# Last attention of a two-block kernel: who merges the dilated groups' weights, and when queries are squared

## The reference

```python
DILATED_GROUPS = ((128, 1), (512, 4), (2048, 16))   # window, dilation
q = rms_norm(h, norm_g) @ w_in                       # 4 heads x 3 groups of 128
q = apply_rope(rms_norm(q, qnorm_g), cos, sin)
for g, (window, dilation) in enumerate(DILATED_GROUPS):
    # query t attends t, t-r, t-2r, ..., t-window of the shared keys
    o_g, l_g = dilated_window_attention(q[:, :, g], k, v, window, dilation)
wts = softmax(stack(l_g)); o = sum_g wts_g * o_g
y = o * silu(z); out = y @ w_out
```

## Time and profile before

| | |
|---|---|
| median of three runs | 1362.85 us |
| profiled execution, device time | 1362.37 us |
| its span, first to last instruction | 1360.6 us |
| PE busy | 1347.0 us, 99% |
| DVE, ACT, POOL busy | 843.6, 631.9, 183.2 us |
| PE idle, 1150 to 1200 us | 3.53 us |
| PE idle, 1200 to 1250 us | 0.00 us |
| PE idle, 1250 to 1300 us | 0.73 us |

### The profile page before, as it was taken

The page is one execution under the profiler, slowest core; times in us unless marked ns, Lnnn a source line. Parts: engine busy times, 40 slices in busy tenths (PEclk is TensorE's granted clock), DMA queues, the critical chain, the costliest instruction groups (busy, mean ns, idle before and its releaser), DMA issues.

```text
span 1360.6 us, 17787 instructions
## 1 busy us (share of the span) xinstructions
PE 1347.0 (99%) x7004; PEld 1101.7 (81%) x7004; DVE 843.6 (62%) x1243; ACT 631.9 (46%) x1006; POOL 183.2 (13%) x167
## 2 busy tenths in 40 slices
PE   9999999999999999999999999999999999999998
PEld 7778787888888788888888888888888888777787
DVE  6565666855344797524767457747464676767685
ACT  5264433433245464323444345444654554477751
POOL 0300010222222200000000112011201120133230
PEclk9999999999999999999999999999999999999999
DMA  6322222323252433332332324422125232221132
GB/s 215 122 79 78 79 78 63 93 69 101 96 181 66 139 118 105 110 102 78 97 105 93 109 78 155 146 87 78 63 71 175 80 118 92 85 71 62 49 139 78
DMA packets 37820, 136.20 MB, mean 100 GB/s; under 512 B 4452, under 2 KB 5476, under 8 KB 37096
## 3 DMA queue, kind: packets, MB, share of 16 engines
q1 hardware_dynamic: 37440, 134.00, 31.1%
q10 hardware_dynamic: 296, 1.06, 0.2%
HBM read 128.74 MB, written 6.30 MB: 99 GB/s over the span
## 4 chain that ended last, share of the span: by engine, by line
PE 88%; DVE 8%; ACT 2%; issue 2%; DMA 1%; POOL 0%; DVEq 0%; SPq 0%; ACTq 0%; POOLq 0%
PE ps L205 85%; PE ps L209 2%; DVE WL L152 2%; DVE TT L164 2%; DVE HL L164 1%; DMA kept<-PW 1%; DVE X L152 1%; DVE sm L170 0%; DVE KT L164 0%; DMA raw<-in_wall 0%; ACT HH L202 0%; DVE gS L164 0%; ACT row L202 0%; ACT SQ L202 0%; ACT WH L189 0%
## 5 line engine op out<-in xcount | busy, mean ns | idle before, releaser
L205 PE MATMUL ps<-HH,WH 128*128 128x512 f32 (+1 forms) x1096 | 435.5, 399 | 1.0 <-DVE HL L164 0.6
L205 PE MATMUL ps<-HL,WH 128*128 128x512 f32 (+1 forms) x1096 | 423.8, 388 | 0.0
L205 PE MATMUL ps<-HH,WL 128*128 128x512 f32 (+1 forms) x1080 | 418.3, 389 | 0.0
L152 DVE TENSOR_TENSOR WL<-raw,WH 128x1024 fp32r<-128x1024 f32 (+1 forms) x221 | 281.6, 1279 | 78.6 <-ACT WH L189 74.5
L189 ACT CAST WH<-raw 128x1024 fp32r<-128x1024 f32 (+1 forms) x222 | 231.0, 1042 | 122.3 <-PE ps L205 99.7
L205 PEld LDWEIGHTS ps<-HH,WH 128*128 128x128 f32 x1096 | 206.2, 188 | 47.8 <-issue 5.0
L205 PEld LDWEIGHTS ps<-HL,WH 128*128 128x128 f32 x1096 | 206.6, 188 | 40.6 <-issue 1.2
L205 PEld LDWEIGHTS ps<-HH,WL 128*128 128x128 f32 x1080 | 203.1, 188 | 42.9
L205 PE MATMUL ps<-PH,WH 128*128 128x512 f32 x424 | 167.1, 394 | 0.0
L205 PE MATMUL ps<-PH,WL 128*128 128x512 f32 x424 | 165.2, 390 | 0.0
L205 PE MATMUL ps<-PL,WH 128*128 128x512 f32 x424 | 165.1, 389 | 0.0
(11 more groups left out here) (234 smaller groups left out, 1466.1 us busy)
## 6 DMA issues: line engine op xcount, KB each, us to landing
raw<-in_wall SPq DMA_DIRECT2D x221, 512.0 KB, 3.6
kept<-PW SPq DMA_DIRECT2D x2, 2048.0 KB, 8.8
PWR<-kept SPq DMA_DIRECT2D x2, 2048.0 KB, 7.8
X<-in_xT SPq DMA_DIRECT2D x8, 256.0 KB, 3.8
X<-in_xT SPq DMA_DIRECT2D x4, 512.0 KB, 5.1
out_T<-X SPq DMA_DIRECT2D x7, 256.0 KB, 2.0
pe<-in_pT SPq DMA_DIRECT2D x2, 512.0 KB, 4.5
MB<-mrow ACTq DMA_DIRECT2D x1, 1024.0 KB, 5.9
```

What stands on the lines that cost most here:

```text
L152: return self.put(None if self.e is None else self.e.tensor_tensor(out, x, y, op))
L205: return self.put(None if self.e is None else self.e.matmul(out, l, r, start=start, stop=stop, skip_group_check=True))
```

## The change

Four things change, all in this stretch:

1. `merge(i)` moves to DVE and takes in the other two steps. DVE adds the two dilated groups straight into the spread places of `PB`, in four instructions of 32 partitions each, and then adds `PB` to the dense weights. ACT's four copies and POOL's two additions of each pair go. POOL only clears `PB` once, when the first exponential is done.
2. For every query tile ACT's square comes first and DVE's products wait for it (`rope sq`); DVE's last product frees the bank.
3. `KC` is made by POOL.
4. After the root of each head ACT takes the exponential of one column of ones, so that the table of the exponential is loaded there.

```diff
@@ pe_program
-                    p.wait_ge(S.act, "kc", h)
+                    p.wait_ge(S.pool, "kc", h)
-                    p.wait_ge(S.pool, "aw", i)
+                    p.wait_ge(S.dve, "aw", i)
@@ v_rope_q
-            if name == ("q", 0, 0):
-                v_turned(v, name, u, ps(*name), gn, S.act, "rope sq", name)
-            else:
-                v_turned(v, name, u, ps(*name), gn, S.pe, *name)
+            v_turned(v, name, u, ps(*name), gn, S.act, "rope sq", name)
...
-            v.then_inc(("rope u", name), *([free(name)] * (name == ("q", 0, 0))))
+            v.then_inc(("rope u", name), free(name))
@@ dve_program, attend
+                def merge(i):
+                    L, W0, tot = att_sizes(SEQ[i][1])
+                    Sc = SS[i % 2]
+                    w = L // 4
+                    v.wait_ge(S.act, "aexp", i)
+                    if i == 0:
+                        v.wait_ge(S.pool, "no class")
+                    else:
+                        v.wait_ge(S.pe, "at", i - 1)
+                    for k in range(4):
+                        r = slice(32 * k, 32 * k + 32)
+                        v.tensor_tensor(PB[r, k:L:4], Sc[r, W0:W0 + w], Sc[r, W0 + w:tot], ADD)
+                    v.then_inc(("spread", i))
+                    v.wait_ge(S.dve, "spread", i)
+                    v.tensor_tensor(Sc[:, 0:W0], Sc[:, 0:W0], PB[:, L - W0:L], ADD).then_inc(("aw", i))
...
+                merge(0)
                 for i in range(16):
-                    if SEQ[i][1] == 3:
-                        shares(SEQ[i][0])
...
+                    if i < 15:
+                        merge(i + 1)
+                        if SEQ[i + 1][1] == 3:
+                            shares(SEQ[i + 1][0])
                     yield
@@ a_rope_q
-            if name == ("q", 0, 0):
-                a.wait_ge(S.pe, *name)
-            else:
-                a.wait_ge(S.dve, "rope u", name)
-            a.activation(by_class(sq_("rope", name)), by_token(ps(*name)), ACT.Square)
-            a.then_inc(("rope sq", name), *([free(name)] * (name != ("q", 0, 0))))
+            a.wait_ge(S.pe, *name)
+            a.activation(by_class(sq_("rope", name)), by_token(ps(*name)), ACT.Square).then_inc(("rope sq", name))
...
                 a.activation(q_rs(h), q_rs(h), ACT.Sqrt).then_inc(("q sqrt", h))
+                a.activation(sm[:, 120:121], ones[:, 0:1], ACT.Exp)
@@ act_program
-                def spread(i):
...
-                    for k in range(4):
-                        r = slice(32 * k, 32 * k + 32)
-                        a.copy(PB[r, k:L:4], SS[i % 2][r, W0:W0 + L // 4])
-                    a.then_inc(("spread", i))
...
-            def key_classes(h):
-                a.wait_ge(S.dve, "kt", h)
-                a.copy(KC[:, h, :].rearrange("p (c j) -> p c j", c=4), KT[:, h, :].rearrange("p (j c) -> p c j", c=4)).then_inc(("kc", h))
@@ pool_program
-                g.tensor_tensor(Sc[:, W0:W0 + w], Sc[:, W0:W0 + w], Sc[:, W0 + w:tot], ADD).then_inc(("ac", i))
...
-                g.tensor_tensor(Sc[:, 0:W0], Sc[:, 0:W0], PB[:, L - W0:L], ADD).then_inc(("aw", i))
...
+                g.wait_ge(S.act, "aexp", 0)
+                g.memset(PB, 0.0).then_inc("no class")
...
+            def key_classes(h):
+                g.wait_ge(S.dve, "kt", h)
+                g.tensor_copy(KC[:, h, :].rearrange("p (c j) -> p c j", c=4), KT[:, h, :].rearrange("p (j c) -> p c j", c=4)).then_inc(("kc", h))
```

More of the change, by code:

```diff
@@ L2546, in attend @@
                 yield
-                spread(0)
                 for i in range(16):
@@ L2558, in attend @@
                     turn(i)
-                    if i < 15:
-                        spread(i + 1)
                     yield
@@ L2801, in q_proj @@
                     a.tile(8)
-                    if 3 * h + g < 4:
-                        key_classes(3 * h + g)
                     a.rope(("q", h, g), a_rope_q(a, h, g), 3 if g == 2 else 2)
@@ L3004, in attend @@
                     yield
-                classes(0)
+                g.wait_ge(S.act, "aexp", 0)
+                g.memset(PB, 0.0).then_inc("no class")
                 yield
                 for i in range(16):
-                    merge(i)
-                    if i < 15:
-                        classes(i + 1)
                     if i < 15:
@@ L3027, in q_proj @@
                     g.tile(8)
+                    if 3 * h + i < 4:
+                        key_classes(3 * h + i)
                     g.rope(("q", h, i), g_rope(g, "q", h, i), 3 if i == 2 else 2)
```

## The result

The changed kernel takes 1371.33 us (median of 5 runs, 1370.04 to 1372.68), the kernel before 1362.85 (1362.12 to 1363.37, 5 runs beside them): 1.0062 times as long, 95% interval 1.0047 to 1.0077. The change makes the kernel slower by 8.5 us. I had forecast 1364.4 and a range of 1359.0 to 1368.0, so the time lies 3.3 us outside. The profiled execution took 1371.16 us, its span 1369.0.

A forecast was written before the change was run, and what follows sets the result against it. PE, busy 99% of the span, was taken as the bound, so only its waits count. Terms -3.8 + 0 + 2.8 + 1.3 + 2.0 - 0.7 = +1.6 us on 1362.37 gave 1364.0, as median 1364.4; range 1359.0 to 1368.0.

The forecast's parts named there:

- mechanism: In query tiles, DVE's products wait for ACT's square, queued behind an exponential awaiting DVE's scores; DVE idles some 2 us.
- step 5: Gate tiles, attention's end: last pair's merge and reciprocal skip POOL and ACT, so waits of 0.5 and 0.2 us go.
- Squares first: Tile (0,1): PE's 2.2 us wait for ACT's square and 1.6 us of slow clock go, 3.8 us gained.
- Step 1: From the squares of (0,2) to turn(0): PE waits 1.1 us there, as before, and stays 3.8 us ahead.
- Steps 2 to 4: DVE's chain makes PE wait at tiles (2,1), (2,2) and (3,2): 2.8, 1.3 and 2.0 us.
- Additions: DVE's merges, four 32-partition additions without overlap plus the add to dense weights: 1.1, 1.35, 1.45, 1.6 us for n = 0 to 3.
- my upper bound of 1.3: Merge(3) and merge(5) beside POOL's `QT`: 0.7 us charged at merge(3); at most 1.3 us at both.
- Table ahead: Load of 1.28 us moves from the scores' path to the products' path: no gain, both lead to the same pair.
- Key copies: ACT loses four key copies; they did not stand where PE waits, so no gain was counted.
- the clock rival: After the wait at tile (3,2) PE drops to its lower clock, costing 1.6 us: 1366.0 to 1366.7, chance 0.30.
- The cover: DVE and ACT chain is shorter than walked, no new waits, only the old one goes: 1358.3, chance 0.22.
- the late squares: ACT still squares (0,1) late, the 3.8 us stay and new waits shrink: 1364 to 1366, chance 0.05.

The follow-up runs named there:

- sq_end: The changed kernel with ACT's square of each query tile issued at the tile's end, ahead of cast and exponential: 1366.04 us, 1.0023.
- one_add: The changed kernel with one addition of 128 partitions per merge in place of four of 32, so its weights differ: 1363.49 us, 1.0005.
- sq_only: The kernel before with ACT's squares ahead of DVE's products in every query tile; merge, key copies and table load as before: 1365.72 us, 1.0022.
- no_table: The changed kernel without the one-column exponential, so the table loads behind the square as before: 1368.18 us, 1.0036.
- end_zg: The changed kernel with three DVE products of gate tiles 2 and 3 moved ahead of the last merge: 1369.18 us, 1.0049.
- merge_only: The kernel before with only the merge moved to DVE: 1373.48 us, 1.0074.
- no_sq: The changed kernel with ACT's squares behind DVE's products again: 1368.38 us, 1.0039.
- kc_act: The changed kernel with the four key copies back on ACT: 1372.59 us, 1.0070.
- merge_sq01_tk: The changed kernel with the square ahead of the products only in tile (0,1) and, as before, (0,0): 1368.30 us, 1.0035.

## Why the prediction was wrong

Its mechanism is shown, by `sq_end` for the order and by the `one_add` pair for the additions; `sq_only` shows that the order costs 4.8 us even without them, there by way of POOL's merge. It fell on step 5 and on the size of several terms. How late PE is against the kernel before, with the 1.3 us of the start taken off (rows above against the earlier trace rows; the last at 1317.08, the squares of the next norm):

| PE's squares | forecast | measured |
|---|---|---|
| (0,2), 1185.42 | -3.8 | -4.0 |
| (1,2), 1210.14 | -3.8 | -2.2 |
| 1217.48 | -1.0 | +0.3 |
| 1243.10 | +0.3 | +3.5 |
| behind the attention | +1.6 | +7.1 |

*Squares first, -3.8:* right. The wait and the slow clock of the earlier trace rows went.

*Step 1, turn(0):* it waits 1.76 us, not 1.1. Memset and merge come 0.6 us later than walked. With 0.26 us for `TH` at (2,0) and 0.36 for a square, 1.6 us of lead was gone where I had 3.8 whole.

*Steps 2 to 4:* the three waits stand where forecast, 1.69, 1.26 and 1.18 us for 2.8, 1.3 and 2.0, and the idle time of DVE is as walked (1.84 for 2, 2.52 for 2.5). The two that are shorter are so because PE was already late. What I missed are small waits between them: turn(5) 0.41, another square 0.36, ACT's copy `PT` for the values 0.48. Between 1217.48 and 1243.10 PE lost 3.2 us, forecast 1.3. A wait of 0.36 us also moves the next start by 0.52 (0.75 from start to start, where 0.23 is usual), since the wait is counted from the end that the profile shows, 0.39 us behind the start; the walk counted waits alone.

*Additions:* a merge alone took some 1.1, 1.5, 1.75 and 1.93 us, from its start to the next instruction's, where I took 1.1, 1.35, 1.45 and 1.6: one addition is 0.20 us at 32 columns and 0.38 at 128, where my slope gave 0.19 and 0.29. Beside `QT` merge(3), merge(5) and merge(9) lost 0.94, 1.04 and 0.76 us; I charged 0.7 once. The price lies between my 0.7 and my upper bound of 1.3, at more places. The Trainium skill ("SBUF — State Buffer", section "SBUF: two separate sides") makes the port that the two share an exclusive lock, which the one that starts first keeps for its whole instruction. The trace agrees in the main: the second addition of merge(3), 0.38 us alone, took 1.32 us, and `QT` had 1.08 us left when it started. The loss is what is left of `QT`, less than the nearly 1.3 us that the prediction drew from the page. The rule that the prediction named beside the additions ("VectorE: DVE Perf Modes", section "Two Vector instructions with no wait between them" of the Trainium skill) agrees too: four additions on different partitions take 1.55 us, four times the 0.385 of one, with no overlap.

*Table ahead, 0:* wrong by 3.2 us, by `no_table` (4.7 up to 1268.77 us of the profiles). "No gain, since both lead to the same pair" overlooked that the scores' path had the load in idle time, and the products' path has none. I had the 1.5 us in the walk three times, but set nothing against it.

*Key copies, 0:* 1.3 us better on POOL than on ACT at most, 0.7 in the profiles up to 1268.77 us; a difference this small stays open.

*Step 5, -0.7:* this step failed. I took the end of the attention for free because no query tile competes there. But the merge stands in DVE's queue ahead of the product that frees a bank, and ahead of two that ACT's cast and copy wait for. PE waited 2.67 us; from 1268.77 to 1317.08 it lost 2.0 us, where I had a gain of 0.7: 2.7 us off, the largest miss. By `end_zg`, with 2.2 us less, nearly all of it was order. With the 1.9 us between 1217.48 and 1243.10 (the small waits that no step has) and the 1.8 us between (0,2) and (1,2) (turn(0) and behind) that is more than the 5.5 us that the stretch is off; the other parts came out 0.9 us below the forecast.

*Rivals:* the clock did not fall behind (3,2) or the end wait in this execution, so the clock rival's way was wrong though its side was right. The cover and the late squares fell with the waits for `TH` and with the first row of PE's timeline.

## What to carry to other kernels

Before moving split work to another engine, count instructions, not elements: four additions on 32 partitions cost four full ones, and a copy that ACT spreads over partitions while it is idle is cheaper than a sum that DVE does four times. Making an engine the first reader is a gain only where its queue is empty ahead of it; of this change the gain lay in one tile, (0,1), and the table load (1358.9), and the load is worth 1.6 us with the square last and costs 3.2 us with the square first. Prices of parts hold only beside the other parts: the merge cost 9.4 us in one order and 2.5 in the other. For each instruction that is put into a queue, list what stands behind it up to the end of the stage, also where the stage seems to have room.

## What the runs showed of the hardware

The length of a wait does not say whether PE's clock falls behind it. Nearly the same wait at the end was followed by full speed in three kernels (2.67 us in the changed one and `merge_only`, 2.68 in `no_sq`) and by the lower clock, 0.43 us from one matmul to the next, in four (2.63 us in `no_table`, `kc_act` and `sq_end`, 2.64 in `merge_sq01_tk`). From 1268.77 to 1317.08 us `kc_act` lost 3.4 us, the changed kernel 2.0. PE in `merge_sq01_tk` behind that wait, 0.43 us apart:

```profile
1295.06 0.63 PE L205 MATMUL ps<-PL,WH 128*128 128x512 f32 x1
1295.49 0.63 PE L205 MATMUL ps<-PH,WL 128*128 128x512 f32 x1
```

The same holds for a shorter wait. That of 1.69 us at tile (2,1) was followed by full speed in the changed kernel and by the lower clock in `end_zg`, which is the same program up to there:

```profile
1213.06 0.63 PE L205 MATMUL ps<-HH,WH 128*128 128x512 f32 x1
1213.49 0.63 PE L205 MATMUL ps<-HL,WH 128*128 128x512 f32 x1
```

That cost 1.2 us at 1212 us, and at tile (2,2), where PE then waited 0.28 us instead of 1.26, it was taken back, since PE would have stood there anyway: what the clock costs depends on whether a wait comes behind it.

In `one_add` the add-back `SS<-SS,PB`, 0.42 us alone, took 1.33 us beside `QT`: what DVE loses to POOL falls on whichever two-input instruction stands there.
